# Expert weights in 16 KB pieces, and the down product with its weights stationary, in a streaming encoder step

## The reference

```python
def expert_block(args):
    xb, e = args
    return (jax.nn.silu(xb @ lp['w1'][e]) * (xb @ lp['w3'][e])) @ lp['w2'][e]
...
x = x + moe(rms_norm(x, lp['g_ffn']), lp)   # each token: two of 32 experts, weighted by its gates
```

## Time and profile before

| | us |
|---|---|
| median of 3 runs | 1584.23 |
| lowest and highest | 1581.51, 1584.6 |
| the profiled execution | 1581.9 |
| its span, first to last instruction | 1580.1 |
| TensorE busy (share of the span) | 1438.2 (91%) |
| VectorE, ScalarE, GpSimd busy | 483.0, 296.6, 203.8 |
| first and last scatter (L1354) issued at | 983.60, 1568.86 |

### The profile page before, as it was taken

One profiled execution on the slowest core, in us unless ns is written; L12 is line 12 of the kernel. 1 busy time (PEld: TensorE's weight loads), 2 busy tenths in 40 slices (PEclk: granted clock), 3 DMA queues, 4 the chain that ended last, 5 costly groups with the idle time before them and its releaser, 6 DMA issues. The chain is left out here.

```text
span 1580.1 us, 29898 instructions
## 1 busy us (share of the span) xinstructions
PE 1438.2 (91%) x12716; PEld 985.3 (62%) x12716; DVE 483.0 (31%) x1002; ACT 296.6 (19%) x634; POOL 203.8 (13%) x291
## 2 busy tenths in 40 slices
PE   5899999659998999999999838999999999999996
PEld 2444444236667667768677427777777777777773
DVE  3100100266456557647455461111111111111110
ACT  5201010133323233334332100000000001000000
POOL 3100000022022112101020001111111111111110
PEclk9999999868978999999999859999999999999998
DMA  7021211421011101101101068999999999999992
GB/s 274 14 78 39 77 39 51 145 73 45 24 52 61 68 22 47 68 21 48 60 3 41 27 219 285 356 363 358 362 365 357 363 360 366 370 358 354 361 365 87
DMA packets 110091, 277.63 MB, mean 176 GB/s; under 512 B 8952, under 2 KB 12920, under 8 KB 110028
## 3 DMA queue, kind: packets, MB, share of 16 engines
q1 hardware_dynamic: 102864, 255.33, 44.7%
q0 software_dynamic: 7168, 21.51, 5.4%
HBM read 248.40 MB, written 32.05 MB: 177 GB/s over the span
## 5 line engine op out<-in xcount | busy, mean ns | idle before, releaser
L916 PE MATMUL psum<-arena 128*64 128x96 f32 x8192 | 355.6, 246 | 14.4 <-DMA arena<-in_w 11.6
L916 PEld LDWEIGHTS psum<-arena 128*64 128x64 f32 x8192 | 345.6, 136 | 22.8 <-issue 18.6
L689 PE MATMUL psum<-arena 128*128 128x512 f32 (+1 forms) x576 | 238.1, 574 | 0.6 <-DVE arena L1424 0.6
L940 PE MATMUL psum<-arena 128*96 128x512 f32 x512 | 227.5, 596 | 0.8 <-issue 0.8
L689 PEld LDWEIGHTS psum<-arena 128*128 128x128 f32 x576 | 108.8, 190 | 124.2 <-issue 124.2
L940 PEld LDWEIGHTS psum<-arena 128*96 128x96 f32 x512 | 80.6, 162 | 124.2 <-issue 120.5
L784 PE MATMUL psum<-arena 128*128 128x512 f32 x288 | 130.4, 607 | 0.8 <-issue 0.8
L643 PE MATMUL psum<-ident,arena 128*128 128x128 f32 (+1 forms) x468 | 76.0, 312 | 59.0 <-DVE arena L1518 27.1
L846 PE MATMUL psum<-arena 128*128 128x64 f32 (+3 forms) x848 | 110.1, 274 | 1.5 <-DVE arena L498 0.8
L643 PEld LDWEIGHTS psum<-ident,arena 128*128 128x128 f32 (+1 forms) x468 | 62.2, 155 | 78.8 <-DVE arena L1518 28.8
L846 PEld LDWEIGHTS psum<-arena 128*128 128x128 f32 (+3 forms) x848 | 101.7, 189 | 8.8 <-issue 1.8
(11 more groups left out here) (218 smaller groups left out, 1303.9 us busy)
## 6 DMA issues: line engine op xcount, KB each, us to landing
arena<-in_w SPq DMA_DIRECT2D x96, 2048.0 KB, 20.0
arena<-in_x_rows SPq DMA_DIRECT2D x18, 512.0 KB, 5.2
z_rows<-arena SPq DMA_DIRECT2D x9, 980.0 KB, 4.5
arena<-in_w_in SPq DMA_DIRECT2D x1, 7840.0 KB, 23.2
arena<-z_rows SPq DMA_DIRECT2D x9, 768.0 KB, 5.2
out_y<-arena SPq DMA_DIRECT2D x9, 512.0 KB, 2.6
xn_rows<-arena SPq DMA_DIRECT2D x9, 512.0 KB, 2.9
arena<-in_w_out SPq DMA_DIRECT2D x1, 4096.0 KB, 17.1
```

The source lines that it names most:

```text
L689: ins = pe.matmul(o[:, 0:hi - lo], xT[s][:, k, :], w_in[:, k, lo:hi], start=(k == 0), stop=(k == KD - 1))
L916: ins = pe.matmul(o[c:c + CT, j * EB:(j + 1) * EB], w[:, k, j * P + c:j * P + c + CT], x[:, k, :], start=(k == 0), stop=(k == KD - 1))
L940: ins = pe.matmul(bank(5 + c)[0:EB], hT[:, k * EB:(k + 1) * EB], w2s[s][:, k, c * BANK:(c + 1) * BANK], start=(k == 0), stop=(k == KF - 1))
```

## The change

The weights w1, w3 and the router's w_route are put on the partitions by another rule: rows p * 8 + k lie on partition p, so that a partition reads one run of 16 KB of w1 or w3. For this, xn is written with its columns in the matching order, which leaves the transposed tiles as the products need them. w2 keeps its rule.

`down` takes w2 as the stationary operand, in two tiles of 64 columns like the up products, and hT moves, 96 columns. Its result is transposed, y features on the partitions, in banks 4 and 5. VectorE copies it to SBUF (`yT_take`, tile yT), and TensorE transposes it back into banks 6 and 7 (`turn_back`), from where `y_take` reads. The loads of w2 wait for yT_full; y_full now comes from `turn_back`, which stands behind `hidden_3`.

```diff
@@ load_expert, load_part
-                                                (row_down, w2s[s], "w2", signals[2], y_full)):
+                                                (row_down, w2s[s], "w2", signals[2], yT_full)):
...
-            eng.dma_start(dst, rows.rearrange("(k p) n -> p k n", p=P)).then_inc(signal, 16)
+            form = "(k p) n -> p k n" if src == "w2" else "(p k) n -> p k n"
+            eng.dma_start(dst, rows.rearrange(form, p=P)).then_inc(signal, 16)
@@ SP
-            sp_.dma_start(w_route, T["w_route"].rearrange("(k p) n -> p k n", p=P)).then_inc(wout_in, 16)
+            sp_.dma_start(w_route, T["w_route"].rearrange("(p k) n -> p k n", p=P)).then_inc(wout_in, 16)
@@ TensorE: down, and the new turn_back
+                pe.wait_ge(yT_ok, b)
+                for j in range(KD):
+                    o = bank(4 + j // 4)
+                    for k in range(KF):
+                        for c in range(0, P, CT):
+                            ins = pe.matmul(o[c:c + CT, (j % 4) * EB:(j % 4 + 1) * EB],
+                                            w2s[s][:, k, j * P + c:j * P + c + CT], hT[:, k * EB:(k + 1) * EB],
+                                            start=(k == 0), stop=(k == KF - 1))
+                ins.then_inc(yT_full, 1)
+
+            def turn_back(b):
+
+                pe.wait_ge(yT_ok, b + 1)
                 pe.wait_ge(y_read, b)
-                for c in range(2):
-                    for k in range(KF):
-                        ins = pe.matmul(bank(5 + c)[0:EB], hT[:, k * EB:(k + 1) * EB],
-                                        w2s[s][:, k, c * BANK:(c + 1) * BANK], start=(k == 0), stop=(k == KF - 1))
+                for j in range(KD):
+                    ins = pe.transpose(bank(6, 2)[0:EB, j * P:(j + 1) * P], yT[:, j], ident[:])
                 ins.then_inc(y_full, 1)
...
                     hidden_3(s, b, w3_in[s], now)
+                    turn_back(b - 1)
             hidden_1(1, NE - 1, w1_in[1], 16 * (NE // 2))
             down(0, NE - 2, w2_in[0], 16 * (NE // 2))
             hidden_3(1, NE - 1, w3_in[1], 16 * (NE // 2))
+            turn_back(NE - 2)
             down(1, NE - 1, w2_in[1], 16 * (NE // 2))
+            turn_back(NE - 1)
@@ ScalarE: y_take
-                act.activation(ye[s][0:EB], bank(5, 2)[0:EB], ACT.Copy, scale=gate_col(col)[0:EB]).then_inc(y_read, 1)
+                act.activation(ye[s][0:EB], bank(6, 2)[0:EB], ACT.Copy, scale=gate_col(col)[0:EB]).then_inc(y_read, 1)
@@ VectorE: xnorm, hidden, the new yT_take and its place
-                    STT(xn, xres, rs_x, g_ffn, ALU.mult, ALU.mult).then_inc(xn_ok, 1)
+                    by_row = lambda a: a.rearrange("p (q k) -> p q k", k=KD)
+                    STT(xn.rearrange("p (k q) -> p q k", k=KD), by_row(xres), rs_x, by_row(g_ffn), ALU.mult,
+                        ALU.mult).then_inc(xn_ok, 1)
...
                 dve.wait_ge(h3_full, b + 1)
+                dve.wait_ge(yT_full, b)
+                STT(hT, uu, 0.5, bank(3)[:, 0:KF * EB], ALU.mult, ALU.mult).then_inc(hh_ok, 1)
+
+            def yT_take(b):
+
+                dve.wait_ge(yT_full, b + 1)
                 dve.wait_ge(y_full, b)
-                STT(hT, uu, 0.5, bank(3)[:, 0:KF * EB], ALU.mult, ALU.mult).then_inc(hh_ok, 1)
+                dve.tensor_copy(yT.rearrange("p (a k) t -> p a (k t)", a=2),
+                                bank(4, 2).rearrange("p (a r) -> p a r", a=2)[:, :, 0:4 * EB]).then_inc(yT_ok, 1)
...
                     silu(b)
+                    yT_take(b - 1)
                     xeT_take(1 - s, b + 1)
                     hidden(b)
             silu(NE - 1)
+            yT_take(NE - 2)
             hidden(NE - 1)
+            yT_take(NE - 1)
```

More of the change, by code:

```diff
@@ L307, in build @@
         hT = A(KF * EB)
+        yT = A(KD, EB)
         ye = [A(D) for _ in range(2)]
@@ L408, in build @@
         y_full, y_read = sem("y_full"), sem("y_read")
+        yT_full, yT_ok = sem("yT_full"), sem("yT_ready")
         ye_out = [sem(f"ye{i}_store") for i in range(2)]
@@ L611, in _ @@
                     load_expert(sp_, 2 * j + s + 2, s, (w1_in[s], w3_in[s], w2_in[s]), 2 * j + s + 1)
-            sp_.wait_ge(y_full, NE)
+            sp_.wait_ge(yT_full, NE)
             total = sp_.value_load(over_e[0:1, MAX_OVER:MAX_OVER + 1], min_val=0, max_val=MAX_OVER)
@@ L968, in _ @@
                         down(0, NE + j, ov_w, 48 * j + 48)
+                        turn_back(NE + j)
         @block.scalar
@@ L1865, in _ @@
                         hidden(NE + j)
+                        yT_take(NE + j)
 def kernel(**inputs):
```

## The result

The change made the kernel slower: 1622.3 us, median of 4 runs (1621.1 to 1633.8), against 1583.1 (1581.5 to 1584.6) before; the ratio is 1.026, 95% interval 1.023 to 1.029. The forecast was 1573 us, range 1556 to 1606. The profiled execution took 1621.1 us (span 1619.3), 39.2 more than that of before.

The account below looks back on a forecast made before the run. TensorE (18.56 us a cycle) and the DMA engines (19.30) were both taken to stand near their limit. 30 cycles at 18.7 instead of 19.07 save 11.1 us, the end 0.8, xnorm costs 0.5: 11.4 less, 1573 us, range 1556 to 1606.

Parts of the forecast that it names:

- The sum of TensorE: Expert loop: three products of 5.43 us, transposes 0.76 and 1.0, tiling changes 0.15; 18.2 us a cycle against 18.56.
- The chain from y_full: y_take, then GpSimd's copy, scatter, copy and next gather: 4.9 us to the gather's issue, with 10.9 us before TensorE stops.
- the end: After the last expert's hidden_3: 8.6 us against 7.84, but an earlier down 1.5 faster, so 0.8 us less.
- the merged pieces: Loads of w1 and w3: neighbouring runs become one 16 KB packet of 604 ns, against 696 for eight of 2 KB.
- Which G?: Expert loop: choice of the gather's landing time after y_full between 9.4 and 13.5 us; 11.3 to 11.5, cycle 18.7 us.
- G: Time from y_full to the gather's landing; if over 10.9 us TensorE stops and the cycle is this time plus 7.2 us.
- the drained queue: DMA queues in the loop: weights end 8.7 us after y_full, then scatter and gather have the engines alone for 2.6 us.
- its own sign of being wrong: Expert loop: the forecast is wrong if the gather's landing doesn't fall below 7 us although weights stop being the limit.
- the gather comes late, and it is slower: Rival, chance 0.28: gather lands 12.0 us or more after y_full, cycle 19.2 us or more; 1606 half way, 1633 full.
- The terms of the sum: Whole kernel: 30 cycles save 11.1 us, the end 0.8, xnorm costs 0.5; 11.4 us less.
- The term for xnorm: Ahead of the loop: xn's strided write costs 0 to 1.3 us, 0.5 taken, as TensorE waits only for the last of nine.
- The pieces' 1.3 us: Loads of w1 and w3: 16 KB pieces cut the DMA engines' need from 19.30 to 18.0 us a cycle.

Follow-up runs that it names:

- e1: The changed kernel, but GpSimd issues the gather of expert b+2 ahead of the scatter of b-1: 1596.6 us, ratio 1.007.
- e7: The changed kernel with 2 KB pieces, xnorm and w_route as before, and GpSimd's scatter one block later, behind the next gather: 1580.5 us, ratio 0.997.
- e13: The changed kernel with 4 KB pieces, scatter one block later, xn written permuted in two halves, contiguous gather transposes: 1576.5 us, ratio 0.994.
- e4: The changed kernel with 2 KB pieces, xnorm and w_route of before, so the new down and turn_back alone: 1616.8 us, ratio 1.019.
- e12: The changed kernel with 14 unread products between down and the gather transposes, to keep TensorE busy: 1617.9 us, ratio 1.020.
- e5: The changed kernel with scatter one block later, xn in natural order, w_route as before, gather transposes reading columns 8 apart: 1577.8 us, ratio 0.994.
- e8: The changed kernel with 4 KB pieces of w1 and w3, scatter one block later, natural xn, transposes of columns 2 apart: 1565.2 us, ratio 0.987.
- e10: The kernel before with 4 KB pieces, xn in natural order and gather transposes of columns 2 apart: 1574.0 us, ratio 0.996.
- e11: The changed kernel with 2 KB pieces, xnorm and w_route of before, and turn_back moved ahead of hidden_3: 1592.4 us, ratio 1.010.
- e2: The changed kernel with turn_back moved ahead of hidden_3, so that y_full comes 5.5 us earlier: 1642.0 us, ratio 1.038.
- e3: The kernel before with the change's 16 KB pieces, xnorm and w_route; down as it was: 1594.5 us, ratio 1.003.
- e6: The kernel before with 16 KB pieces, xn in natural order and strided gather transposes; down as it was: 1582.7 us, ratio 0.997.

## Why the prediction was wrong

**What held.** The sum of TensorE: down in 5.4 us (1264.45 to 1269.9), turn_back in 1.01, gather transposes in 0.81, 18.1 to 18.2 us in all where nothing is waited for (e1, e7, e13). The parts without any change of tiling made 18.05, so at most 0.15 us is left for the two more. The chain from y_full over four steps of GpSimd to the gather, and that it would close on itself, held; so did the kind of wait (gather, none for weights), the end (8.7 us from hidden_3 on, 8.6 forecast: turn_back 1.0, down 5.6, copy 1.07, turn_back 1.0), and the merged pieces. From 1258.5 to 1261 us only 16 KB packets ran, and 0.993 x 16 x 2500/65 = 611 ns each, 604 forecast:

```profile
q1 hardware_dynamic: 65, 1.06, 99.3%
```

**The step that failed is "Which G?"**: w2, w1 and w3 were to end 8.7 us after y_full, and scatter and gather then to have the engines alone, for G = 11.4 and a cycle of 18.7. In the cycle shown, the three issues on SP's queue landed thus (w2 and w1, then w3, minimum, median and maximum of each pair or single):

```profile
DMA to landing us min/median/max: 8.0/10.0/12.0
...
DMA to landing us min/median/max: 11.4/11.4/11.4
```

w2, issued at 1250.73, landed at 1258.7; w1 at 1263.6, 12.9 us after the first issue where 1.6 + 10.1 = 11.7 were reckoned; w3, issued at 1258.15, at 1269.55, 10.4 after y_full. The scatter was not waiting its turn behind them but running among w3's pieces: from 1264 to 1269 us packets of GpSimd's queue took a quarter of the engines' time,

```profile
q0 software_dynamic: 92, 0.28, 25.7%
```

and w3 ended 2.3 us after the 1267.3 that the forecast's own terms give from w2's issue (1250.73 + 1.6 + 5.25 + 9.7). When w3 was done the rest did not fill the engines: the DMA shares of 1250 to 1275 us in slices of 0.625 us are 7, 7, 7, 5 tenths from 1269.4 to 1271.9.

```profile
DMA  2109599999999999999999999997989777597999
```

The forecast divided the packets' time by full engines, and took the order of issue for the order of service. Its G of 11.4 gave the gather 6.5 us from issue to landing; the median is 7.4, and 12.3 after y_full. So the drained queue came only in part, and the landing did not fall below the 7 us that the forecast had named as its own sign of being wrong. 12.3 us after y_full is on the far side of the 12.0 us that the rival "the gather comes late, and it is slower" named as its deciding point. That rival happened, between its half-way price (19.8 us a cycle, 1606) and its full one (20.7, 1633). At 0.28 it was given too little: the rows stood 7.5 to 9.9, and only an argument stood against them. Its second reason, pieces of 604 ns in the gather's way, was not needed: e4 closes the loop with 2 KB pieces and lands its gathers in 7.5 us.

**What no step had.** A TensorE that stands 0.6 to 2.5 us in nearly every cycle fell to its lower clock in 8 of them, 13 us. e12 takes all falls but one away with the chain left as it is, and the cycle becomes 19.73; e1 and e7 take the waits away, and from 1000 us on no fall is left.

**The terms of the sum.** A cycle came out 1.51 us over the 18.7 of the forecast, whose terms gave 18.6: 0.9 for the landing, 0.2 for what lies outside it (7.4 for 7.2), 0.45 for the falls. 29 x 1.51 = 43.8 us.

The term for xnorm, 0.5 us, was mis-sized too: the first gather transposes start 7.9 us later. Only the last of nine xnorms was to be on the path. Beside the earlier trace rows, in the timeline of after:

```profile
911.42 1.96 DVE L1653 SCALAR_TENSOR_TENSOR arena<-arena,small 128x1024 f32<-128x1024 f32 x1 [2.20 <-POOL small L1272]
...
913.44 1.97 PE L646 MATMUL psum<-ident,arena 128*128 128x128 f32 x8 [4.95 <-DVE arena L1653]
```

It takes 1.96 us, 0.68 more, and starts 6.3 us later than in before. Eight stand ahead of it, and eight times 0.68 is 5.4; but they were not all paid. From the fourth xnorm to the fifth after takes 0.7 us more than before (58.7 and 58.0), from the seventh to the eighth as long (70.2 in both). Of the eight traces with xn written contiguously the first gather is issued at 945.5 to 954.3 us, of the five with the strided write at 953.8 to 966.9; the means are 948.7 and 960.8. Beside the strided write all five have w_route's rows of the change. How these 12 us divide between the two, and how much of them is chance, is open.

Together 43.8 + 7.4 (a start 7.9 later, 0.5 forecast) is 51.2 us; the gap in the profiled executions is 39.2 + 11.4 = 50.6. The 0.6 lies at the loop's ends.

**The pieces' 1.3 us.** The packets' time per cycle, share times cycle from 1000 to 1500 us, is (0.799 + 0.128) x 20.21 = 18.7 us in after, where before has (0.899 + 0.137) x 19.07 = 19.8: 1.0 us less, so the term is near. But after's DMA engines have time to spare, and there it buys nothing. With the loop open it bought little in e1: the lead lasted longer, but the pace behind it was 19.5 us, with gathers that take 14 us; e5, with the same pieces and gathers of 12 us, held 18.4. What sets e1's 19.5 is not shown. 4 KB pieces, with landings of 8.4 to 8.6 us, have cycles of 18.5 to 18.8 in the mean (e8, e10, e13).

**Still open:** why e1's pace is 19.5 us once the lead is used up, where e5's stays at 18.4 for 27 cycles; the length of the attention stage, which differs by 9 to 13 us between profiled executions with the same code there; and, maybe with it, some 10 us of the medians of e11, e12 and e13.

## What to carry to other kernels

When a result gets an extra step on the engine that is the bound, follow what is triggered by it, over every queue, back to that engine: here GpSimd issued the next gather behind the scatter, and a y_full that came one hidden_3 and one turn_back later left 10.9 us for a chain of 12.3, where there had been 18.6. That closed a loop of 19.7 us. Breaking it by one reordered issue (e1, e7) was worth 26 to 36 us, more than the 11 us that the change was forecast to bring. Size DMA pieces by the slowest small transfer beside them, and take issue to landing from rows of the loop itself, not from a drained queue that the forecast only hopes for.

## What was not expected of the hardware

- Beside pieces of 16 KB an indirect gather takes 12 to 14.3 us in the median (e1, e2, e3, e5, e6), where beside 2 KB and 4 KB pieces it takes 8.4 to 8.6 (before, e7, e8, e10, e11, e13). In after, with 16 KB pieces but a DMA share of 0.93, it is 7.4, and in e4, with 2 KB pieces, 7.5. (The Trainium skill, DMA: Bandwidth & Descriptors, Queues, rings and completion order, says that a DMA engine takes turns between its queues packet by packet; the longer landings beside 16 KB pieces fit that, but from 2 KB to 4 KB, 8.5 or 8.6 and 8.4 to 8.6 us, nothing of it shows.)
- Idle times of 1.6 to 2.5 us in a 20 us cycle were enough for the granted clock to fall to its lower level for some 3.4 us, in 8 of 29 cycles of after. Other waits as long (1.80, 1.99 and 2.42 us among them) had no fall behind them, nor had any shorter one. With waits up to 3.6 us (e2) it fell in 14, with waits up to 2.7 us (e4) in 12.
- A 128x1024 scalar_tensor_tensor takes 1.96 to 2.00 us where it writes with a stride of 512 B, 1.28 contiguous.
- Eight 96x128 transposes whose stationary columns lie 2 or 8 apart take 1.20 (e8) and 1.13 us (e5), contiguous 0.88 (e7); beside the old down it is 1.08 (e10) and 1.02 (e6), contiguous 0.82.
